# Modulation weights loaded in pieces whose partitions interleave two or four column blocks, in a fused two-model kernel

## The chip, the cores and the metric

The kernel runs on one core of a Trainium2 chip. The metric is the device time of one execution in microseconds (us). The core has a matrix engine (PE), a vector engine (DVE), a scalar engine (ACT), GpSimd (POOL) and a sync engine (SP) that issues most of the transfers (DMAs). The engines run beside each other and wait for each other on semaphores.

## The reference

Two transformer-like blocks follow each other on a sequence of 256 tokens of width 1024, in fp32. The first has two layers of feed-forward, token mixing and feed-forward; the second has one attention layer and one recurrent layer, each with a large feed-forward. What matters here is the modulation: every layer scales, shifts and gates its activations with vectors that come from one conditioning vector.

```python
c_act = jax.nn.silu(c)
mod = c_act @ ada_w[l] + ada_b[l]      # [1024] @ [1024, 9 * 1024]
sh1, sc1, g1, sh2, sc2, g2, sh3, sc3, g3 = jnp.split(mod, N_MOD, axis=-1)
h = modulate(rms_norm(x, norm_ffn1[l]), sh1, sc1)
# second block: 6 * 1024 columns a layer, for two vectors
mx = jnp.split((silu_c @ ada_w[i] + ada_b[i])[:, None, :], N_MOD_2, axis=-1)
mc = jnp.split(silu_cc @ ada_w[i] + ada_b[i], N_MOD_2, axis=-1)
```

Each of these products reads 1024 x 1024 weights for a segment (one `sh1`, `sc1` and so on), 4 MB, and uses every weight once for each vector.

## The kernel before

All weights pass through one stream of loads. `plan` lists the units (a unit is 1 MB of ordinary weights, mostly 1024 rows by 256 columns) in the order in which PE uses them, and `due` says before which unit each modulation segment must be complete. `build` cuts every segment into four pieces of 1 MB: 512 rows (four tiles of 128 rows) by 512 columns, first both row halves of the left 512 columns, then of the right. A budget over the units, with each unit's room, spreads the pieces between them; each piece costs as many steps as it has vectors. The result is `stream`, 271 units and 126 pieces.

SP walks through `stream` and loads each entry into one of four buffers `raw`, as soon as the entry four places before has been taken (semaphore `taken`). An ordinary unit is split in two parts: ACT copies it to the rounded high part `wh`, DVE subtracts to get the low part `wl`. PE then makes three products for each tile (high by high, high by low, low by high). ACT and DVE work up to two units ahead of PE.

A piece is handled on DVE alone (`take`, line 2108 for the multiply-add, line 2104 for the first step, a scale). For each of its four row tiles DVE adds, on every partition, the tile's 512 columns times that partition's element of the silu of the vector, into one of three sums `ACC` of 128 partitions by 512 columns. So a piece is four DVE steps for each vector, and a sum of 512 columns is complete after two pieces. For a few segments of the second block both vectors are taken in one pass.

PE then sums over the partitions (`flush`): four products, each with 128 columns of `ACC` as the weights and a column of ones as the moving side, give 512 results as four columns of the PSUM bank `PB[7]`. An fp32 product of this kind shows as two records in the trace. `summed` notes when a sum is complete and flushes older ones if more than three would be open, `spent` flushes after a unit until two are pending, and `mods` flushes all that a segment needs just before it is used. DVE then adds the bias (`mod`).

The start is special: of the first segment the right half is multiplied by PE itself (`direct_cols`), the small vectors are transposed by PE (the ring `su`) and copied by ACT, and then come the first three flushes, the first modulation and the first pair of units.

All helper calls of PE have line 623, those of DVE 2100 to 2108, those of ACT 1461 and 1462, the loads of SP line 568.

Of the kernel before, what the change touches and what calls it, by code (L numbers as in the profile page):

```python
# [27 lines left out]
K_MAIN = 385  # L28
K_R2, K_D0, K_D1, K_RD0, K_RD1, K_COS, K_SIN, K_BAND = 385, 513, 641, 769, 897, 1025, 1281, 1537
K_ALL = 2049  # L30
# [180 lines left out]

class Side:
# [24 lines left out]
def build(nc, t, out):  # L237
    units, due = plan(t)
    adas, direct = [], []
    for seg in sorted(due, key=lambda s: (due[s], s)):  # L240
# [3 lines left out]
        for i in range(4):  # L244
            src = w[512 * (i % 2):512 * (i % 2) + 512, s * 1024 + (i // 2) * 512:s * 1024 + (i // 2) * 512 + 512]
            if seg == (0, 0, 0):

                if i // 2:
                    direct.append(src)
                    continue  # L250
            adas.append((seg, i, vecs, due[seg], src))
# [13 lines left out]
    cost = np.cumsum([len(a[2]) for a in adas])  # L265
    ends = {}
    for a, c in zip(adas, cost):
        ends[a[3]] = c
    stream, ai, budget, sent = [], 0, 0.0, 0
    for i, u in enumerate(units):  # L270
        rate = max([(c - budget) / max(room[d] - room[i], 0.1) for d, c in ends.items() if d > i] + [0.0])
        budget = max(budget + max(rate, 0.0) * (room[i + 1] - room[i]), ends.get(i, 0))
        while ai < len(adas) and (cost[ai] <= budget + 1e-6 or adas[ai][3] <= i):
# [11 lines left out]
    for p, (kind, u) in enumerate(stream):  # L285
        seen[p % RAW] += 16 * (len(u[3]) if kind == "w" else 1)
# [3 lines left out]
        elif u[1] % 2:  # L290
            for v in u[2]:
                COLS_AT[(u[0][0], v, u[0][1], u[0][2])] = COLS_AT[None] = COLS_AT.get(None, 0) + 1
# [28 lines left out]
    with ExitStack() as ctx:  # L321
# [49 lines left out]
        IDB = sb("IDB", [128, 128], BF16)  # L371

# [21 lines left out]
        VR = [Y[:, i, 0:128] for i in range(4)]  # L394

# [105 lines left out]

        def smc(c, n):
# [45 lines left out]
        def _(e):  # L548
# [8 lines left out]
            for p, (kind, u) in enumerate(stream):  # L557
# [8 lines left out]
                parts = [(0, 4, 0, 512, u[4])] if kind == "a" else u[3]  # L566
                for k0, kn, c0, cn, src in parts:
# [35 lines left out]
        def _(e):  # L603
# [27 lines left out]
            def flush():  # L631

                p, v, i, key = pend.pop(0)
                E.wait_ge("taken", p + 1)
                E.wait_ge("mod", E.n["mod"])
                c0 = SEGCOL[key] + 4 * (i // 2)
# [4 lines left out]
                columns.append((key, c0))  # L641
                flushed[0] += 1

            def summed(places):
                for p in places:
                    kind, u = stream[p]
                    if kind == "a" and u[1] % 2 == 0:
                        acc[0] += len(u[2])
                        while flushed[0] < acc[0] - ACCS:
                            flush()  # L650
                    elif kind == "a":
                        pend.extend((p, v, u[1], (u[0][0], v, u[0][1], u[0][2])) for v in u[2])
# [802 lines left out]
        def _(e):  # L1455
# [104 lines left out]
            def ffn(l, seg, first=None):  # L1560
# [534 lines left out]
        def _(e):  # L2095
# [22 lines left out]
            def take(places):  # L2118

                for p in places:  # L2120
# [8 lines left out]
                    seg, i, vecs, _, _ = u  # L2129
                    view = raw_view(p)  # L2130
                    E.wait_ge(f"raw{p % RAW}", LAND[p])
                    E.wait_ge("su.read", 1)
                    base = sums_of[0]
                    for k in range(4):
                        for x, v in enumerate(vecs):
                            a = ACC[:, (base + x + 1) % ACCS, :]
                            col = 8 * v + 4 * (i % 2) + k
                            c = CV[:, col:col + 1]
                            if k == 0 and i % 2 == 0:
# [5 lines left out]
                            if k == 3 and v == vecs[-1]:  # L2145
# [4 lines left out]
                    if i % 2:  # L2150
                        sums_of[0] += len(vecs)
# [310 lines left out]
            E.step(e.memset(EPSC, EPS))  # L2462
            take(range(0, 3))
# [474 lines left out]
```

## Time and profile before

| | before |
|---|---|
| time, median of 3 runs | 2228.17 us (2224.69 to 2229.52) |
| span of the profiled execution | 2222.6 us |
| PE busy | 2155.5 us (97%) |
| DVE busy | 1674.6 us (75%) |
| ACT busy | 990.5 us (45%) |
| bytes moved | 417.47 MB, mean 188 GB/s |
| loads of modulation weights | 126 of 1 MB |

The profile is of one execution, and its span leaves out what lies around it, so it is compared with other spans. An engine's busy share is a mean over stages with different limits: the first feed-forwards carry many modulation pieces, the attention in the middle carries none. "Busy" for PE is modelled and hides gaps shorter than the length of a product, so a PE at 100% may still differ in pace.

### The profile page before, as it was taken

How to read it: one execution, taken by the hardware profiler on the slowest of the kernel's cores; microseconds unless marked ns; L12 is line 12 of the kernel's file. 1: busy time of each engine (PE TensorE's matmuls, PEld its weight loads, DVE VectorE, ACT ScalarE, POOL GpSimd, SP SyncE). 2: the span in 40 equal slices, each digit the busy share in tenths (PEclk: the TensorE clock that was granted, in tenths of full speed). 3: DMA queues.
4: the chain of work that ended last, by engine and by line, in shares of the span. 5: the costliest groups of instructions: out<-in, count | busy, mean ns of one | idle time of the engine just before them, and what ended most of it. 6: DMA issues, size and time to landing. Idle time of an engine off the chain costs nothing.

```text
span 2222.6 us, 36384 instructions
## 1 busy us (share of the span) xinstructions
PE 2155.5 (97%) x15539; PEld 1993.2 (90%) x15539; DVE 1674.6 (75%) x2327; ACT 990.5 (45%) x1331; POOL 31.1 (1%) x33
## 2 busy tenths in 40 slices
PE   7999999999999999999999899999999999999998
PEld 7999987999999998799998678888888887889998
DVE  6999877788798877778776774777776568987563
ACT  4534434534443443443344664422222348764442
POOL 0000000000000000000000000000000001110000
PEclk9999999999999999999999999999999999999999
DMA  9999744798789864467774102254465232133662
GB/s 322 317 330 309 248 133 150 242 316 298 264 284 305 302 202 153 142 196 248 236 228 142 36 4 74 80 186 155 156 221 189 76 114 69 48 122 127 223 191 76
DMA packets 338631, 417.47 MB, mean 188 GB/s; under 512 B 9274, under 2 KB 263208, under 8 KB 338472
## 3 DMA queue, kind: packets, MB, share of 16 engines
q1 hardware_dynamic: 335360, 411.84, 56.2%
q10 hardware_dynamic: 3112, 3.33, 0.5%
q8 instruction: 122, 2.00, 0.4%
q14 instruction: 37, 0.30, 0.0%
HBM read 414.09 MB, written 1.05 MB: 187 GB/s over the span
## 4 chain that ended last, share of the span: by engine, by line
PE 46%; DVE 7%; ACT 3%; issue 2%; POOL 0%; DVEq 0%; ACTq 0%
PE pb L623 45%; ACT wh L1461 1%; DVE wl L2100 1%; DVE T L2108 1%; PE pb L1289 1%; DVE ACC L2108 1%; DVE SM L2694 1%; DVE RS L2192 0%; DVE Hl L2108 0%; DVE L_y L2108 0%; ACT A_P L1935 0%; DVE L_y L2100 0%; ACT L_y L1462 0%; DVE L_y L2815 0%; DVE L_u L2108 0%
## 5 line engine op out<-in xcount | busy, mean ns | idle before, releaser
L623 PE MATMUL pb<-Hh,wh 128*128 128x256 f32 (+1 forms) x2624 | 795.5, 304 | 13.8 <-DVE wl L2100 5.4
L623 PE MATMUL pb<-Hl,wh 128*128 128x256 f32 (+1 forms) x2624 | 779.3, 297 | 0.0
L623 PE MATMUL pb<-Hh,wl 128*128 128x256 f32 (+1 forms) x2624 | 774.7, 297 | 0.0
L2100 DVE TENSOR_TENSOR wl<-raw,wh 128x2048 fp32r<-128x2048 f32 (+3 forms) x271 | 600.9, 2222 | 179.9 <-ACT wh L1461 179.1
L1461 ACT ACTIVATE wh<-raw 128x2048 fp32r<-128x2048 f32 (+3 forms) x271 | 502.2, 1855 | 357.6 <-PE pb L623 259.0
L623 PEld LDWEIGHTS pb<-Hh,wh 128*128 128x128 f32 x2624 | 504.6, 192 | 33.5 <-issue 9.6
L623 PEld LDWEIGHTS pb<-Hl,wh 128*128 128x128 f32 x2624 | 504.9, 192 | 15.3 <-issue 2.2
L623 PEld LDWEIGHTS pb<-Hh,wl 128*128 128x128 f32 x2624 | 501.9, 192 | 12.8
L623 PE MATMUL pb<-Bh,wh 128*128 128x256 f32 (+1 forms) x1376 | 420.1, 305 | 7.1 <-DVE Y L2100 2.5
L623 PE MATMUL pb<-Bl,wh 128*128 128x256 f32 (+1 forms) x1376 | 413.5, 300 | 0.0
L623 PE MATMUL pb<-Bh,wl 128*128 128x256 f32 (+1 forms) x1376 | 413.4, 300 | 0.0
L2108 DVE SCALAR_TENSOR_TENSOR ACC<-raw,SM,ACC 128x512 f32<-128x512 f32 x525 | 381.6, 750 | 18.1 <-DMA raw<-in_ada_w_dram 6.8
L623 PEld LDWEIGHTS pb<-Bh,wh 128*128 128x128 f32 x1376 | 263.3, 191 | 19.4 <-issue 6.4
L623 PEld LDWEIGHTS pb<-Bl,wh 128*128 128x128 f32 x1376 | 263.3, 191 | 9.3 <-issue 0.5
L623 PEld LDWEIGHTS pb<-Bh,wl 128*128 128x128 f32 x1376 | 263.2, 191 | 8.8
L1461 ACT ACTIVATE Bh<-T 128x512 fp32r<-128x512 f32 x92 | 58.1, 632 | 278.7 <-DVE T L2100 278.7
L1462 ACT ACTIVATE T<-pb 128x512 f32<-128x512 f32 x92 | 54.7, 595 | 159.0 <-PE pb L623 158.0
L2100 DVE TENSOR_TENSOR Bl<-T,Bh 128x512 fp32r<-128x512 f32 x92 | 63.7, 693 | 64.2 <-ACT Bh L1461 64.2
L2100 DVE TENSOR_TENSOR Y<-Y,pb 128x512 f32<-128x512 f32 x68 | 44.9, 684 | 58.7 <-PE pb L623 58.5
L623 PE MATMUL pb<-T,KM 128*128 128x256 f32 (+1 forms) x280 | 78.6, 408 | 3.9 <-ACT T L1462 3.9
L623 PEld LDWEIGHTS pb<-KM,ACC 128*128 128x128 f32 x600 | 74.0, 192 | 1.6 <-issue 0.5
L623 PE MATMUL pb<-KM 128*128 128x256 f32 x302 | 72.5, 390 | 0.0
(256 smaller groups left out, 2113.9 us busy)
## 6 DMA issues: line engine op xcount, KB each, us to landing
raw<-in_ada_w_dram SPq DMA_DIRECT2D x126, 1024.0 KB, 5.5
raw<-in_ffn_w_in_dram SPq DMA_DIRECT2D x88, 1024.0 KB, 6.7
raw<-in_mlp_w_dram SPq DMA_DIRECT2D x64, 1024.0 KB, 5.3
raw<-in_ffn_w_out_dram SPq DMA_DIRECT2D x32, 1024.0 KB, 6.5
raw<-in_mix_w_in_dram SPq DMA_DIRECT2D x22, 1024.0 KB, 5.7
raw<-in_ffn_w_out_dram SPq DMA_DIRECT2D x16, 768.0 KB, 4.6
raw<-in_attn_w_qkv_dram SPq DMA_DIRECT2D x12, 1024.0 KB, 6.2
raw<-in_lru_w_in_dram SPq DMA_DIRECT2D x10, 1024.0 KB, 5.1
```

Of the source, the lines that this page charges most:

```text
L623: return e.matmul(o, l, r, start=st, stop=sp, skip_group_check=True)
L1289: ins = e.transpose(p[:, c], A_P[:, 2 * (s % 2) + x, c], IDN)
L1461: return e.activation(o, i, func, scale=scale)
L1462: return e.activation(o, i, func, bias=bias, scale=scale)
L2100: return e.tensor_tensor(o, a, b, f)
L2108: return e.scalar_tensor_tensor(out=o, in0=a, scalar=s, in1=b, op0=f1, op1=f2)
L2694: E.step(e.tensor_reduce(S_NM2[:, h + x:h + x + 1], PB[S2[n % 2][x]][:, 0:nk], AXX, ALU.max))
```

## The change

A segment is now cut by rows first. A piece still has 1 MB, four `raw` rows of 512 columns on each of 128 partitions, but partition p holds column block p modulo q: with q = 2 both 512-column halves of one segment, with q = 4 the four halves of two neighbouring segments that are due at the same time. Piece i of 2q holds 512/q rows of the weights, and each of its tiles 128/q rows. It is loaded with q transfers, one for each block, to every q-th partition. All pieces of a segment (four) or of a pair (eight) go into one sum of 128 by 512, and PE's flush multiplies by q columns of marks (`K_BLK`, 1 where the partition belongs to the block) instead of one column of ones. The first two segments keep their old pieces (q = 1).

The vectors must be laid out in the same way, as `CW` with 144 columns: after its first small step DVE makes two copies that repeat each element q times, PE transposes six parts of 24 rows, and ACT applies the Silu while copying them to `CW`, after the first modulation. DVE waits for that copy before its first interleaved piece (`su.read` 10).

```diff
+K_BLK = {1: K_ONE, 2: 385, 4: 387}
+    for q in (2, 4):
+        k[p, K_BLK[q] + p % q] = 1.0
@@ build: the list of pieces
-        for i in range(4):
...
+        q = 2
+        if order and order[0] == (b, l, s + 1, *only) and due[order[0]] == due[seg]:
+            order.pop(0)
+            q = 4
+        for i in range(2 * q):
+            rows = w[512 // q * i:512 // q * (i + 1)]
+            adas.append(Piece(b, l, s, 0, q, i, vecs, due[seg], [rows[:, s * 1024 + 512 * j:s * 1024 + 512 * j + 512] for j in range(q)]))
@@ SP: loads
-                parts = [(0, 4, 0, 512, u[4])] if kind == "a" else u[3]
+                if kind == "a":
+                    n = 128 // u.q
+                    for j, src in enumerate(u.parts):
+                        e.dma_start(view[j::u.q, :, :], src.rearrange("(k p) n -> p k n", p=n)).then_inc(sems[f"raw{p % RAW}"], 16)
+                    continue
@@ PE: flush
+                blocks = KM[:, K_BLK[u.q]:K_BLK[u.q] + u.q]
                 for h in range(4):
-                    ins = mm(PB[7][:, c0 + h:c0 + h + 1], ACC[:, a, h * 128:h * 128 + 128], KM[:, K_ONE:K_ONE + 1], True, True)
+                    ins = mm(PB[7][:, c0 + h:c0 + h + 4 * u.q - 3:4], ACC[:, a, h * 128:h * 128 + 128], blocks, True, True)
@@ PE: summed (a sum opens with its first piece and is ready after its last)
-                    if kind == "a" and u[1] % 2 == 0:
+                    if kind == "a" and u.i == 0:
...
-                    elif kind == "a":
...
+                    elif kind == "a" and u.i == 2 * u.q - 1:
+                        pend.extend((p, v, u) for v in u.vecs)
@@ PE: start
+            E.wait_ge("dve.step", 3)
+            pw = fill("su")
+            for a in range(6):
+                z = VW4[:, 128 * a:128 * a + 128] if a < 4 else VW2[:, 128 * a - 512:128 * a - 384]
+                ins = e.transpose(pw[:, 24 * a:24 * a + 24], z, KM[0:24, K_ID:K_ID + 24])
+            full(ins, "su")
@@ ACT: after the first modulation
+                    act(CW[:, :], full("su")[:, 0:144], ACT.Silu).then_inc(sems["su.read"], 1)
@@ c_col: the column of the vector that belongs to tile kk of a piece
+            k, a = divmod(kk, q)
+            if q == 1:
+                return CV[:, 8 * v + k:8 * v + k + 1]
+            c = (0 if q == 4 else 96) + 24 * a + 8 * v + k
+            return CW[:, c:c + 1]
@@ DVE: take
-                    E.wait_ge("su.read", 1)
+                    E.wait_ge("su.read", 1 if u.q == 1 else 10)
...
-                            if k == 0 and i % 2 == 0:
+                            if k == 0 and u.i == 0:
                                 E.wait_ge("cols", base + x + 1 - ACCS)
                                 ins = ts(a, view[:, 0, :], c, None, ALU.mult, None)
@@ DVE: start
+            E.wait_ge("l_c", 64)
+            for q, z in ((4, VW4), (2, VW2)):
+                E.step(e.tensor_copy(z.rearrange("r (p q) -> r p q", q=q), VR[1][0:24, :].unsqueeze(2).to_broadcast([24, 128, q])))
```

## Rows read from the trace of the kernel before

**Rows 1.** Page, parts 1 and 5: busy us, instructions; mean ns of one

```profile
PE 2155.5 (97%) x15539; PEld 1993.2 (90%) x15539; DVE 1674.6 (75%) x2327; ACT 990.5 (45%) x1331; POOL 31.1 (1%) x33
...
L2100 DVE TENSOR_TENSOR wl<-raw,wh 128x2048 fp32r<-128x2048 f32 (+3 forms) x271 | 600.9, 2222 | 179.9 <-ACT wh L1461 179.1
```

**Rows 2.** Stretch: us; busy PE, PEld, DVE, ACT, POOL; clock, DMA, GB/s

```profile
94.00:181.00 87.00, 87.00 (x732) 87.00 (x731) 81.31 (x95) 35.59 (x30) 0.00 (x0) 1.00 0.98 330
181.00:250.00 69.00, 67.01 (x539) 66.39 (x539) 65.81 (x84) 27.26 (x27) 0.00 (x0) 0.98 0.92 307
...
410.00:611.00 201.00, 200.54 (x1665) 200.10 (x1666) 166.13 (x182) 80.92 (x69) 0.00 (x0) 1.00 0.89 299
611.00:835.00 224.00, 223.79 (x1856) 222.89 (x1855) 186.08 (x213) 97.83 (x93) 0.00 (x0) 1.00 0.82 273
```

**Rows 3.** Waits of 410 to 611 us: total, times, longest

```profile
ACT wh L1461 <- PE pb L623: 35.7, 10, 4.7
```

**Rows 4.** DVE's waits of 94 to 181 us; its scales on `ACC`

```profile
DVE Bl L2100 <- ACT Bh L1461: 3.5, 5, 0.7
DVE wl L2100 <- ACT wh L1461: 0.5, 1, 0.5
...
L2104 DVE TENSOR_SCALAR ACC<-raw,SM x12: 386/480/486, 98.9 to 242.3; 128x512 f32<-128x512 f32 x12
```

**Rows 5.** Timeline of PE, its first wait for `wl`

```profile
195.24 0.38 PE L623 MATMUL pb<-Hh,wh 128*128 128x256 f32 x1 [1.35 <-DVE wl L2100]
```

**Rows 6.** Instructions on the tile `ACC`, whole span

```profile
L623 PE MATMUL pb<-KM,ACC x600: 164/250/353, 33.5 to 2184.1; 128*128 128x1 f32 x150
L2108 DVE SCALAR_TENSOR_TENSOR ACC<-raw,SM,ACC x525: 740/752/769, 8.1 to 2168.6; 128x512 f32<-128x512 f32 x175
L2104 DVE TENSOR_SCALAR ACC<-raw,SM x75: 386/481/494, 7.6 to 2127.7; 128x512 f32<-128x512 f32 x75
```

**Rows 7.** Timeline of PE around a flush: start, length, what

```profile
335.14 0.28 PE L623 MATMUL pb<-wh,Hl 128*128 128x256 f32 x1
335.26 0.95 PE L623 MATMUL pb<-KM,ACC 128*128 128x1 f32 x8
...
336.27 0.28 PE L623 MATMUL pb<-wl,Hh 128*128 128x256 f32 x1
```

**Rows 8.** The same for PE's products on `ACC` alone; (x) counts records

```profile
94.00:181.00 87.00, 6.87 (x60) 1.00 0.98 330
181.00:250.00 69.00, 4.29 (x37) 0.98 0.92 307
...
410.00:611.00 201.00, 8.51 (x72) 1.00 0.89 299
611.00:835.00 224.00, 11.35 (x96) 1.00 0.82 273
```

**Rows 9.** Timeline of PE: the two flushes at the seam near 2000 us

```profile
2000.85 1.84 PE L623 MATMUL pb<-KM,ACC 128*128 128x1 f32 x16
```

**Rows 10.** Timelines of the start: PE, PE, ACT

```profile
26.96 0.63 PE L1105 MATMUL pb<-KM,Y 128*128 128x128 f32 x4
...
33.51 3.20 PE L623 MATMUL pb<-KM,ACC 128*128 128x1 f32 x24
...
51.50 0.60 ACT L1462 ACTIVATE T<-pb 128x512 f32<-128x512 f32 x1 [3.33 <-PE pb L623]
```

**Rows 11.** SP's issues of the gate weights, and their time to landing

```profile
1789.73 0.37 SPq L568 DMA_DIRECT2D raw<-in_lru_w_a_dram  x1
...
1791.17 0.47 SPq L568 DMA_DIRECT2D raw<-in_lru_w_i_dram  x1
...
DMA to landing us min/median/max: 2.8/3.3/3.7
```

**Rows 12.** SP's load of 1 MB just before them

```profile
DMA to landing us min/median/max: 5.4/5.4/5.4
```

**Rows 13.** DMA rate of 0 to 222 us in 40 slices

```profile
GB/s 145 387 376 387 387 359 348 163 287 378 357 291 364 139 288 365 324 358 323 361 281 368 342 362 340 281 372 273 374 311 367 360 225 369 191 339 347 209 374 306
```

More of the change, by code:

```diff
@@ L1 @@
 import itertools
-from collections import defaultdict
+from collections import defaultdict, namedtuple
 from contextlib import ExitStack
@@ L27 @@
 K_ID, K_ONE, K_R1, K_INVF = 0, 128, 256, 384
-K_MAIN = 385
-K_R2, K_D0, K_D1, K_RD0, K_RD1, K_COS, K_SIN, K_BAND = 385, 513, 641, 769, 897, 1025, 1281, 1537
-K_ALL = 2049
+K_BLK = {1: K_ONE, 2: 385, 4: 387}
+K_MAIN = 391
+K_R2, K_D0, K_D1, K_RD0, K_RD1, K_COS, K_SIN, K_BAND = 391, 519, 647, 775, 903, 1031, 1287, 1543
+K_ALL = 2055
 def constants():
@@ L209 @@
 LO_FULL = {j: 2 * LO_STEPS.index((j, 1)) for j in range(4)}
+Piece = namedtuple("Piece", "b l s half q i vecs due parts")
 class Side:
@@ L239, in build @@
     adas, direct = [], []
-    for seg in sorted(due, key=lambda s: (due[s], s)):
+    order = sorted(due, key=lambda s: (due[s], s))
+    while order:
+        seg = order.pop(0)
         b, l, s, *only = seg
@@ L243, in build @@
         vecs = only or ([0] if b == 0 else ([1, 2] if l == 0 or s < 2 else [1]))
-        for i in range(4):
-            src = w[512 * (i % 2):512 * (i % 2) + 512, s * 1024 + (i // 2) * 512:s * 1024 + (i // 2) * 512 + 512]
-            if seg == (0, 0, 0):
-                if i // 2:
+        if seg in ((0, 0, 0), (0, 0, 1)):
+            for i in range(4):
+                src = w[512 * (i % 2):512 * (i % 2) + 512, s * 1024 + (i // 2) * 512:s * 1024 + (i // 2) * 512 + 512]
+                if s == 0 and i // 2:
                     direct.append(src)
                     continue
-            adas.append((seg, i, vecs, due[seg], src))
+                adas.append(Piece(b, l, s, i // 2, 1, i % 2, vecs, due[seg], [src]))
+            continue
[6 more added lines that the diff above has]
+            adas.append(Piece(b, l, s, 0, q, i, vecs, due[seg], [rows[:, s * 1024 + 512 * j:s * 1024 + 512 * j + 512] for j in range(q)]))
     at_unit = [ROOM.get(u[0], 1.0) for u in units]
@@ L264, in build @@
     room = np.concatenate([[0.0], np.cumsum(at_unit)])
-    cost = np.cumsum([len(a[2]) for a in adas])
+    cost = np.cumsum([len(a.vecs) for a in adas])
     ends = {}
     for a, c in zip(adas, cost):
-        ends[a[3]] = c
+        ends[a.due] = c
     stream, ai, budget, sent = [], 0, 0.0, 0
@@ L272, in build @@
         budget = max(budget + max(rate, 0.0) * (room[i + 1] - room[i]), ends.get(i, 0))
-        while ai < len(adas) and (cost[ai] <= budget + 1e-6 or adas[ai][3] <= i):
+        while ai < len(adas) and (cost[ai] <= budget + 1e-6 or adas[ai].due <= i):
             stream.append(("a", adas[ai]))
@@ L285, in build @@
     for p, (kind, u) in enumerate(stream):
-        seen[p % RAW] += 16 * (len(u[3]) if kind == "w" else 1)
+        seen[p % RAW] += 16 * len(u[3] if kind == "w" else u.parts)
         LAND.append(seen[p % RAW])
@@ L289, in build @@
             POS.append(p)
-        elif u[1] % 2:
-            for v in u[2]:
-                COLS_AT[(u[0][0], v, u[0][1], u[0][2])] = COLS_AT[None] = COLS_AT.get(None, 0) + 1
+        elif u.i == 2 * u.q - 1:
+            for v in u.vecs:
+                COLS_AT[None] = COLS_AT.get(None, 0) + 1
+                for s in range(u.s, u.s + (2 if u.q == 4 else 1)):
+                    COLS_AT[(u.b, v, u.l, s)] = COLS_AT[None]
     START, SECOND = POS[0] + 1, POS[1] + 1
@@ L631, in flush @@
             def flush():
-                p, v, i, key = pend.pop(0)
+                p, v, u = pend.pop(0)
                 E.wait_ge("taken", p + 1)
                 E.wait_ge("mod", E.n["mod"])
-                c0 = SEGCOL[key] + 4 * (i // 2)
+                c0 = SEGCOL[(u.b, v, u.l, u.s)] + 4 * u.half
                 a = (flushed[0] + 1) % ACCS
+                blocks = KM[:, K_BLK[u.q]:K_BLK[u.q] + u.q]
                 for h in range(4):
-                    ins = mm(PB[7][:, c0 + h:c0 + h + 1], ACC[:, a, h * 128:h * 128 + 128], KM[:, K_ONE:K_ONE + 1], True, True)
+                    ins = mm(PB[7][:, c0 + h:c0 + h + 4 * u.q - 3:4], ACC[:, a, h * 128:h * 128 + 128], blocks, True, True)
                 ins.then_inc(sems["cols"], 1)
-                columns.append((key, c0))
+                for j in range(u.q):
+                    columns.append(((u.b, v, u.l, u.s + j // 2), c0 + 4 * j))
                 flushed[0] += 1
@@ L2144, in take @@
                                 ins = stt(a, view[:, k, :], c, a, ALU.mult, ALU.add)
-                            if k == 3 and v == vecs[-1]:
+                            if k == 3 and v == u.vecs[-1]:
                                 ins.then_inc(sems["taken"], 1)
```

19 lines of the change are left out of this document (10 added, 9 removed).

## The prediction

> **What bounds the kernel now.** I read the page's busy shares first: PE is busy for 2155.5 of 2222.6 us [rows 1], so PE is the likely bound. A share averages over stages, so the table of stretches comes next [rows 2]. In 410 to 611 us PE is busy 200.54 of 201 us and ACT waits for PE, because its buffers are full [rows 3]: PE sets the pace. In 94 to 181 us PE is just as full, but DVE is busy 81.31 of 87 us, and of its 5.7 us of idle time the largest named part is the hand-over of hidden values from ACT, 3.5 us [rows 4]. DVE never waits for PE there. At 195.24 us PE at last waits 1.35 us for DVE's low half `wl` [rows 5]. In 181 to 250 us DVE is busy 65.81 of 69 us. So from about 94 to 250 us DVE paces the kernel just behind PE, and the reader should see that PE time saved there is not time saved. The profiled execution spans 2222.6 us; the median of the timed runs, 2228.17, is 5.6 us above it, and I carry those 5.6 us over unchanged.
>
> **What is removed on PE.** A sum that is ready in `ACC` costs four fp32 products, eight records [rows 6]. In the stream this is 335.14 to 336.27 us from the matmul before to the second one behind, 1.13 us where two steps of 0.12 would be 0.24: 0.89 us a flush [rows 7]. The 600 records are 75 flushes. For after I go through the planner's list of segments, where two neighbours with one due time become a pair. The first two segments keep their 3. In the rest of the first block, segments 2, 5 and 8 stay alone and (3,4) and (6,7) pair up in both layers, and (0,1) in layer 1: 11. The context columns (0,1) ahead of time: 1. The second block: (0,1) 1, segment 2 twice (two vectors), (3,4) twice, 5 twice, next layer (0,1) twice, (2,3), 4 and 5 once each: 12. Together 3 + 11 + 1 + 12 = 27. So 48 flushes vanish, 48 x 0.89 = 42.7 us of PE time.
>
> Each remaining flush has q = 2 or 4 columns of block marks instead of one column of ones. Records of one column and of 256 columns alike follow each other at about 0.12 us [rows 7], so 2 or 4 columns lie between two equal prices and cost nothing more.
>
> **Where the flushes lie.** PE flushes when more than two sums are pending, or when a segment is asked for. With half as many sums or fewer, most now wait until they are asked for. Of the 75, 3 lie at the start, 8 in four pairs at seams, where PE waits for squares from ACT in any case (one of the pairs: 16 records at 2000.85 us [rows 9]), and 64 inside matmul streams. After: 3 at the start, 11 at seams, 13 inside. The cover of a seam flush is the square and copy that ACT makes of the last tile; were it gone, 11 - 8 = 3 more flushes there cost 2.7 us. Inside streams 64 - 13 = 51 flushes fall away, 45.4 us. Of these, 94 to 250 us holds 60 + 37 records, 12 flushes [rows 8], of which 2 stay. The 10 that go are worth 8.9 us of PE time but nothing in time, because DVE paces that stretch. What is left: 41 x 0.89 = 36.5 us.
>
> **What is added on DVE.** The count of multiply-adds is the same, 600. But a sum's first step was a scale of 481 ns (75 of them) and is otherwise a multiply-add of 752 ns [rows 6]; 48 of them change, 48 x 0.27 = 13 us spread over the run. Where PE paces, DVE has room (166.13 of 201 us busy [rows 2]) and this costs nothing. In 94 to 250 us 12 sums began [rows 4] and 3 will: 9 x 0.27 = 2.4 us straight on the path. Just as close to a limit are the parts of 410 to 835 us with the most modulation work; PE's saving pushes DVE's share in 410 to 611 us from 83% to some 86%, more in its densest parts, and DVE reached 93 to 95% when it paced. I take 1.5 us off, bounds 0 and the 14 us of a rival below.
>
> **What is added at the start.** Two small copies on DVE fit in its first wait for data. PE makes six more transposes ahead of the direct columns; four there take from 26.96 to about 27.4 us, 0.12 each [rows 10], so 0.7 us. They need a bank that ACT frees after its first copy of the vectors, perhaps 0.2 us, and PE's three flushes at 33.51 us [rows 10] end the chain to the first modulation: 0.7 us on the path, bounds 0 and 1.5. DVE's later wait for the copied `CW` has nothing late in it: ACT's one Silu falls before 51.50 us, where ACT has waited 3.33 us for PE [rows 10].
>
> **What moves in the queues.** A piece keeps its 1 MB and its runs of 2 KB, but becomes 2 or 4 transfers of 64 or 32 partitions. SP's issues take 0.37 to 0.47 us, so a piece's last part goes out 0.4 to 1.4 us later. The nearest row is the unit of gate weights, four 256 KB transfers on all partitions: first issued 1789.73, last 1791.17, each landed within 3.7 us, so the unit was in after at most 5.2 us [rows 11], where one 1 MB transfer took 5.4 [rows 12]. So no loss in a quiet queue. Behind a piece on SP stands the next unit's weight load; in the busy stretch DVE frees buffers 2.2 us apart or more, the time of one `wl` [rows 1], longer than four issues. No row shows transfers of 32 partitions spaced by four. Bounds: nothing, or half speed (first rival). I take 1.5 us, nearer to the gate weights' row.
>
> The Trainium skill ("DMA: Bandwidth & Descriptors", Measured and Rules for kernel authors) speaks against the change: at least 1 MiB a transfer for 75% of peak, and disjoint partition halves gain nothing because they serialize. By its fit of 2.0 us plus bytes at 436 GB/s, an estimate, four parts in strict sequence would take 10.4 us instead of 4.4; the gate weights' row disagrees, since the parts overlap. The same skill ("SBUF — State Buffer", Door 1) says that bandwidth follows how many of 16 ports the partitions reach, and every fourth partition reaches all; no row here shows it.
>
> **The sum.** 36.5 - 2.4 - 1.5 - 0.7 - 1.5 = 30.4, rounded down to 29 for seam flushes that may not hide wholly: span 2193.6, time 2199.
>
> **Rivals.** (1) The parts collide: several DMA engines write to the same few partitions' port at once, and a piece moves at c times the time of now. In 94 to 181 us the queues are 98% busy at 330 GB/s, a weight unit and a piece every 6.4 us [rows 2]. The best slices reach 387 GB/s [rows 13], 2.7 us a MB. A pair then takes 2.7 x (1 + c), over 6.4 from c = 1.35. At c = 2 each of 24 pieces in 94 to 250 us adds 1.75 us, 42 us. In 410 to 835 us 121 MB take 313 us at best, the 42 pieces add 114: 427 us instead of 425, so the 16 flushes saved there bring nothing and 2 us are lost. The other 25 flushes still bring 22 us. Total 2228 + 44 - 22 + 1 = 2251. It turns slower than before from about c = 1.9, where 65 x (c - 1.35) equals the 36 us gained. For it: the busy queues; against: equal bytes and run length, and four parts in a row that cost nothing.
> (2) The front end (DVE, with ACT's weights late from DMA) paces 410 to 835 us too once PE is quicker: 16 x 0.89 = 14 us less, 2213. For it: DMA share 0.89 and 0.82; against: ACT waits for PE 35.7 us in 410 to 611 [rows 3].
> (3) All inner flushes are gained, because DVE's pace was partly PE's: 2228 - 45.4 + 0.7 = 2184. Against it: PE's wait at 195 us.
> (4) The change does less than it says: a middling collision, c near 1.8, eats the gain: within 0.2%.
>
> **How the numbers follow.** This kernel can be told from no change beyond about 0.2%, 4.5 us. Forecast 0.58; rival 1 0.14, rival 2 0.14, rival 3 0.06, rival 4 0.08. Faster: 0.58 + 0.14 + 0.06 = 0.78; same 0.08; slower 0.14. The range runs from rival 3, 2185, to the edge of rival 4, 2226, and leaves out rival 1 and some of 4.
>
> **What would show it.** `ACC` products on PE: 216 records, not 600. Stretches after 250 us shorter by 0.89 us for each flush gone; the first 250 us not shorter, perhaps 3 longer, with more PE waits for `wl`. DVE's scales on `ACC`: 27. Landing of pieces near 6 to 7 us in the busy stretch if the queues bear it, 9 and more with DVE waiting for `raw` if they collide. I would be wrong if 32-partition transfers are slow, or if seams wait for the late flushes.

## Result and profile after the change

| | before | after |
|---|---|---|
| time, median of 4 runs each, on one chip | 2226.43 us (2220.85 to 2229.52) | 2211.52 us (2206.09 to 2214.35) |
| ratio, with its 95% interval | | 0.994 (0.9921 to 0.9959) |
| span of the profiled execution | 2222.6 us | 2203.6 us |

The change gains about 15 us. The forecast was 29. The time lies inside the range and the sign is the one forecast, but half of the gain is missing, and most of what follows asks where it went. All figures are from fast runs; one run of the kernel before, at 6412.82 us with a granted clock of 0.326, is left out throughout.

The page of the kernel after, parts 1, 5 and 6; after the bar: busy us, mean ns of one, and idle time before; the loads' last number is the median time from issue to landing in us.

```profile
PE 2119.4 (96%) x15161; PEld 1953.9 (89%) x15161; DVE 1686.0 (77%) x2325; ACT 991.5 (45%) x1332; POOL 31.8 (1%) x33
...
L654 PE MATMUL pb<-KM,ACC 128*128 128x2 f32 (+2 forms) x216 | 27.3, 251 | 1.7 <-DVE ACC L2148 1.7
...
raw<-in_ffn_w_in_dram SPq DMA_DIRECT2D x88, 1024.0 KB, 7.3
raw<-in_ada_w_dram SPq DMA_DIRECT2D x320, 256.0 KB, 4.1
```

PE has 36.1 us less work than in [rows 1], and the products on `ACC` are 216, as forecast. The first block's feed-forward weights (`in_ffn_w_in`) landed 6.7 us after their issue before and take 7.3 now.

The stretches that answer to [rows 2] (same columns):

```profile
94.00:181.00 87.00, 82.46 (x667) 81.50 (x667) 80.33 (x92) 33.28 (x26) 0.00 (x0) 0.98 0.96 324
181.00:250.00 69.00, 60.10 (x479) 58.98 (x478) 65.62 (x84) 27.09 (x26) 0.00 (x0) 0.98 0.90 303
410.00:611.00 201.00, 200.43 (x1657) 199.71 (x1656) 174.12 (x193) 86.94 (x77) 0.00 (x0) 1.00 0.89 299
611.00:835.00 224.00, 222.62 (x1821) 219.52 (x1820) 191.54 (x217) 98.83 (x91) 0.00 (x0) 1.00 0.86 285
```

In the first two rows PE was busy 87.00 and 67.01 us; now it is busy 82.46 and 60.10, while DVE is as full as it was. Freed PE time turned into waiting there. In the last two rows PE is still full: it paces, and what it saved is time saved.

Waits of 94 to 250 us in the kernel after (us in total, times, longest):

```profile
PEld pb L654 <- DVE wl L2140: 14.5, 10, 3.0
PE pb L654 <- DVE wl L2140: 8.7, 7, 2.8
```

Before, the same two came to 1.6 us on PEld (the weight loads) and 1.3 us on PE, the one at 195 us [rows 5].

To see where time is won and lost I laid the executions on top of each other: for each unit of weights, when PE starts on it, and how much later or earlier that is than in the profiled execution of the kernel before. The last columns are for experiments below. "Again" is another profiled execution of the same kernel.

| PE starts unit | before at | before again, twice | after | after again | pieces whole (a4_whole) | late interleaving | again |
|---|---|---|---|---|---|---|---|
| 2, first block | 54.0 | -0.9, -0.6 | +0.4 | +0.3 | +7.7 | +0.9 | +0.5 |
| 8 | 94.6 | -0.9, -0.6 | +0.1 | -0.5 | +6.9 | +0.9 | +0.5 |
| 33 | 249.7 | 0.0, +1.7 | +7.1 | +7.0 | +9.5 | +3.6 | +2.6 |
| 85 | 605.1 | 0.0, +1.7 | -2.6 | 0.0 | +0.1 | -3.2 | -6.1 |
| 120 | 815.3 | -0.1, +1.7 | -8.2 | -6.1 | -6.2 | -9.0 | -12.3 |
| 177, second block | 1209.3 | -1.6, +0.1 | -13.2 | -12.7 | -9.4 | -15.5 | -18.5 |
| 216 | 1709.0 | +1.1, +2.9 | -16.8 | -16.4 | -14.4 | -18.9 | -19.5 |
| 270, last | 2159.4 | -0.6, +1.1 | -18.5 | -18.1 | -16.1 | -20.7 | -21.3 |

The kernel after loses 7 us between units 8 and 33, in 94 to 250 us, and then wins 25.6 to the end. Between these two units executions of the kernel before differ by up to 2.3 us (0, +0.9 and +2.3), so 7 is well outside. What was expected of the two further executions of the kernel before:

> The kernel before, looked at once more, to see how far PE's start of each unit moves between two executions of one kernel. If the first 250 us repeat within 1 us, the 2 to 3 us that most variants lose between 169 and 250 us are an effect of their edits; if they move by 2 to 3 us, that much is the spread of a stretch whose loads are late, and only the 7 us of the changed kernel are more.

### The profile page after: what moved, and what is told of

The parts are those of the page before. It is cut to its first block, busy times and chain, and to the rows that moved or that the text cites. A ratio compares the mean times of both kernels' runs of the same rounds, so it can differ in the third digit from the quotient of the medians.

```text
span 2203.6 us, 35914 instructions
## 1 busy us (share of the span) xinstructions
PE 2119.4 (96%) x15161; PEld 1953.9 (89%) x15161; DVE 1686.0 (77%) x2325; ACT 991.5 (45%) x1332; POOL 31.8 (1%) x33
## 4 chain that ended last, share of the span: by engine, by line
PE 44%; DVE 9%; ACT 3%; issue 2%; POOL 0%; DVEq 0%; ACTq 0%
PE pb L654 43%; DVE ACC L2148 2%; ACT wh L1500 1%; DVE wl L2140 1%; PE pb L1328 1%; DVE T L2148 1%; DVE SM L2735 0%; DVE Hl L2148 0%; DVE RS L2230 0%; DVE L_y L2148 0%; DVE T L2140 0%; DVE L_y L2140 0%; ACT L_y L1501 0%; DVE L_y L2856 0%; DVE L_u L2148 0%
## 5 line engine op out<-in xcount | busy, mean ns | idle before, releaser
L654 PEld LDWEIGHTS pb<-Hh,wl 128*128 128x128 f32 x2624 | 500.3, 191 | 12.7
L2148 DVE SCALAR_TENSOR_TENSOR ACC<-raw,CW,ACC 128x512 f32<-128x512 f32 x552 | 400.2, 749 | 10.8
L1501 ACT ACTIVATE Hh<-T,MOD 128x256 fp32r<-128x256 f32 x104 | 49.4, 504 | 42.3 <-DVE T L2148 42.3
```

What stands on the lines that cost most here:

```text
L654: return e.matmul(o, l, r, start=st, stop=sp, skip_group_check=True)
L1501: return e.activation(o, i, func, bias=bias, scale=scale)
L2148: return e.scalar_tensor_tensor(out=o, in0=a, scalar=s, in1=b, op0=f1, op1=f2)
```

## The experiments

All ratios are to the kernel before on the same chip. "Early loss" is how much later unit 33 starts, less the same of unit 8.

**The split of the pieces, alone** (measured twice). The kernel before; only the loads are cut.

```diff
+                if kind == "a" and p > 5:
+                    for j in range(4):
+                        e.dma_start(view[j::4, :, :], u[4].rearrange("(k p) n -> p k n", p=128)[j::4, :, :]) ...
```

> The kernel before with one thing added: every modulation piece from the seventh stream entry on is loaded with four transfers, each to every fourth partition, with the same bytes to the same places. Layout, sums, flushes and scales are those of before. Theory 1 (the split transfers cost the time that the changed kernel lost in its first 250 us, 7 us there): weights land later behind the split pieces, 8 us instead of 7 from issue to landing in 94 to 250 us, DVE waits for the high halves, and the last unit of that stretch (start 249.7 before) starts 4 to 6 us later; the whole is 4 to 8 us slower, ratio 1.002 to 1.0035. Theory 2 (the multiply-add starts and the start's extra work cost it): nothing lands later that anyone waits for, within 1 us of before.

> The split over every fourth partition once more, beside the other three splits: 1.002 to 1.004 if its cost repeats.

Measured: 1.0032 (1.0014 to 1.005) and 1.0024 (1.0012 to 1.0037), early loss 4.0 and 8.0 us; after unit 33 the two executions keep the same distance to the end, within 2 us. Splitting costs 5 to 7 us by the ratios, and in the profiles all of it falls where the front end (loads, ACT, DVE) paces, and nothing where PE does.

**The split undone.** The kernel after, with each piece in one transfer. What lands then no longer fits the interleaved layout, so its sums mix rows and columns of the weights.

```diff
-                    for j, src in enumerate(u.parts):
-                        e.dma_start(view[j::u.q, :, :], src.rearrange("(k p) n -> p k n", p=n)) ...
+                    e.dma_start(view, u.parts[0].rearrange("(k p) n -> p k n", p=128)) ...
```

> The changed kernel with each piece loaded by one transfer of 1 MB, as before the change (the data then does not fit the interleaved layout: rows and columns of the weights are left mixed up). Everything else is the changed kernel. Theory 1 (split transfers): 5 to 8 us faster than the changed kernel, so 20 to 23 us faster than before, ratio 0.990; weights land in 7 us again in 94 to 250 us, and the last unit there starts 2 to 3 us later than before instead of 7. Theory 2 (starts and start-up): as the changed kernel, ratio 0.993 to 0.994.

Measured: 0.9935 (0.9915 to 0.9955). The early loss falls from 7 us to 2.6, near the spread of the kernel before: theory 1 holds for the early loss. But the ratio is the one of theory 2: the time hardly moves, 2209.47 us against 2211.42 for the kernel after on the same chip. Its profile starts with unit 2 already 7.7 us late, before any interleaved piece; that surprise is taken up below.

**DVE's longer first steps**, alone and undone. Both kernels leave out parts of their sums or add to what was there.

```diff
 a3_starts, in the kernel before:
-                                ins = ts(a, view[:, 0, :], c, None, ALU.mult, None)
+                                if opens(seg[0], seg[1], seg[2], i):
+                                    ins = ts(a, view[:, 0, :], c, None, ALU.mult, None)
+                                else:
+                                    ins = stt(a, view[:, 0, :], c, a, ALU.mult, ALU.add)
 d2_scales, in the kernel after:
+                            elif k == 0 and u.i % 2 == 0:
+                                E.wait_ge(*mine[v])
+                                ins = ts(a, view[:, 0, :], c, None, ALU.mult, None)
```

> The kernel before, where 48 of the sums' first steps on DVE are multiply-adds instead of scales, as many and about at the places where the change makes them so; they add to what the sum held, so the modulation vectors come out of wrong sums. Nothing else moves. Theory A (the prediction's): DVE paces 94 to 250 us, 9 of these steps lie there, 2.4 us longer, ratio 1.001, and nothing elsewhere. Theory B (DVE's longer steps are a good part of the 7 us that the changed kernel loses before unit 33, since a later hand-over of wl goes back into the queues): 5 us or more, ratio 1.002 and up. Theory C: hidden, within 0.5 us.

> The changed kernel, where the first step of every second piece of a sum is a scale again, as many scales as in the kernel before (75); what the sum held is lost there, so the modulation vectors are wrong. Theory A (DVE's longer starts are 2.4 us of the 7 us lost by unit 33, and the split loads the rest): unit 33 comes 4 to 5 us behind the kernel before instead of 7, and the time is 2 to 2.5 us less than the changed kernel's: ratio 0.993. Theory B (only the queues are late there, DVE's steps lie in the shadow of late loads): unit 33 stays 7 us behind, ratio 0.994 to 0.995. Theory C (DVE is the bound alone): all 7 us come back, ratio 0.991.

Measured: 1.001 (0.9997 to 1.0022), early loss 2.1 us, no more than the kernel before shows by itself; and 0.9931 (0.9907 to 0.9955), early loss 7.5 us. Giving DVE its short steps back returns nothing of the early loss. What DVE saved it waited instead. Its wait for ACT in the stretch from unit 8 to unit 33, first in the kernel after (94 to 257 us), then in d2_scales (101 to 265 us):

```profile
DVE wl L2140 <- ACT wh L1500: 2.7, 6, 1.2
```

```profile
DVE wl L2140 <- ACT wh L1500: 5.3, 7, 1.2
```

That is 2.6 us more, where nine short steps save 2.4. So the early loss speaks for theory B of the second text: the steps lie in the shadow of late loads. The ratio alone can't tell, since 0.9931 is what theory A had. The profile of d2_scales also won 32.2 us after unit 33, and not 25.6; it had 34 us at the lower of PE's two clock levels (1.2 of 2.4 GHz) between unit 33 and the last, where the kernel after had 44. Work at half the clock loses half of its time at most, here 5 of the 10 us, and that is most of the difference. No run separates this from an effect of the steps.

**Why the split costs.** Three other ways to cut the same piece, beside the two measurements above.

```diff
 e3_tiles:     view[:, j:j + 1, :]        four transfers, each to all 128 partitions
 e4_quarters:  view[32 * j:32 * j + 32]   four transfers, each to 32 neighbours
 e5_two:       view[j::2, :, :]           two transfers, even and odd partitions
```

> The kernel before, where each piece from the seventh on is loaded in four transfers of 256 KB, one for each row tile, so that every transfer goes to all 128 partitions. Undoing the split gave back most of the changed kernel's early loss; SP's issues took 2.6 us for a piece of four there. Theory N (the number of transfers costs: issues and packets): as slow as the split over every fourth partition, ratio 1.002 to 1.004, SP busy near 2.6 us a piece. Theory G (the shape costs: 32 partitions a transfer): SP's four issues take 1.6 us as those of the gate weights, landing as before, ratio 1.000 to 1.001.

> The kernel before, where each piece from the seventh on is loaded in four transfers to 32 neighbouring partitions each. Theory I (the interleaving costs: partitions four apart): faster than the split over every fourth partition, ratio 1.000 to 1.001. Theory G (32 partitions a transfer cost, wherever they lie): the same as that split, 1.002 to 1.004. Theory P (neighbouring partitions share a port and collide): slower than it, 1.01 or more, pieces landing 9 us or more after their issue.

> The kernel before, where each piece from the seventh on is loaded in two transfers, to the even and the odd partitions. If the cost of the split goes with the number of transfers, half of it: ratio 1.001 to 1.002, SP's two issues 1.3 us. If it is only the place where SP's issues come to more than the 2.2 us between two buffers set free, nothing: 1.000.

| | ratio | early loss | SP's issues of one piece | weights of the first block land after |
|---|---|---|---|---|
| one transfer (before) | 1 | 0 to 2.3 us | 0.37 us | 6.7 us |
| two, every second partition | 0.9998 (0.9984 to 1.0012) | 0.3 | 1.28 | 7.1 |
| four, one for each row tile | 0.9993 (0.9979 to 1.0008) | 2.8 | 1.75 | 7.2 |
| four, every fourth partition | 1.0024 and 1.0032 | 8.0 and 4.0 | 2.6 | 7.5 |
| four, 32 neighbours each | 1.0832 (1.0783 to 1.0881) | 69.6 | 1.74 | 12.1 |

SP's timeline of three kernels, about 163 to 175 us (start, duration of all issues, what, count). First the kernel before:

```profile
169.85 0.37 SPq L568 DMA_DIRECT2D raw<-in_ada_w_dram  x1
172.05 0.37 SPq L568 DMA_DIRECT2D raw<-in_ffn_w_in_dram  x1
```

The kernel after:

```profile
169.79 2.54 SPq L596 DMA_DIRECT2D raw<-in_ada_w_dram  x4
172.38 0.59 SPq L599 DMA_DIRECT2D raw<-in_ffn_w_in_dram  x1
```

And two transfers a piece (e5_two):

```profile
163.54 1.28 SPq L568 DMA_DIRECT2D raw<-in_ada_w_dram  x2
165.74 0.38 SPq L572 DMA_DIRECT2D raw<-in_ffn_w_in_dram  x1
```

An issue to every second or fourth partition takes 0.64 us, one to all partitions or to neighbours 0.44. Two of the first kind, or four of the second, end before the next buffer is free, 2.2 us after the first issue, and cost nothing that can be measured. Four of the first kind take 2.6 us: the weights behind the piece go out at +2.6 instead of +2.2, their own issue takes 0.59 us instead of 0.37, and ACT waits for weights (35.6 us for `in_ffn_w_in` in 94 to 250 us of the kernel after, 31.1 before). So the cost seems to have a threshold, and not to go by the number of transfers. Some 24 pieces at 0.4 us would be 10 us if every one counted; 4 to 8 were seen. This reading is an inference from the first four rows of the table, which agree with it. SP was not delayed by itself, so a slower transfer of the strided parts (the weights land after 7.5 us with it and 7.2 with row tiles) is not excluded.

The last row of the table is the collision of rival 1, in pure form. Slices of its page in this stretch move 221 to 242 GB/s where the kernel before moves 330 [rows 2], at the same byte count, with the DMA engines counted as busy throughout. Its waits in 94 to 250 us:

```profile
ACT wh L1465 <- DMA raw<-in_ffn_w_in_dram: 72.2, 12, 12.0
```

The Trainium skill ("SBUF — State Buffer", Door 1: The DMA port swizzle) says that the bandwidth of a transfer goes by how many of 16 ports its partitions reach. These runs agree: 32 neighbours cost 8.3%, 32 partitions spaced by four 0.2 to 0.3% at equal size. The Trainium skill ("DMA: Bandwidth & Descriptors", Rules for kernel authors) advises against two transfers to disjoint partition halves, because they serialize. Here even and odd halves neither gained nor lost: 0.9998.

**The price of a flush.** The kernel before; 48 of the flushes are cut from four fp32 products to one of four columns, so three quarters of their sums are left out.

> The kernel before, in which 48 of the 75 flushes, those that the change does without, make one product with four columns of ones instead of four products with one (their sums are left out). Loads and DVE's work are those of before. It takes 48 x 0.67 = 32 us of PE time away, three quarters of what the change takes. Theory A (my sum: PE's time inside matmul streams after 250 us is time, flushes at 94 to 250 us are free): 40 x 0.67 = 27 us faster, ratio 0.988. Theory B (PE's time comes back as waits for DVE and lower granted clock, whatever the loads do): 12 to 16 us faster, ratio 0.993 to 0.9945, with as many or more low-clock spells as the changed kernel.

Measured: 0.9912 (0.9887 to 0.9936), 19 us, between the figures of the two theories. PE's start of the last unit comes 25.8 us earlier in the profile, and unit 33 gained nothing. Between these two units the flushes took 23.8 us less. The profile won more than that, 26.7 us, because it was an execution with a high clock: 27 us at the lower level there, where the kernel before had 37 (the mean over the span, as a share of full speed, is 0.991 against 0.987). Up to half of these 10 us is clock and not flushes. So the flushes are worth about what their rows say, where PE paces. And again the median of the runs moved less than the profile: their mean clock was 0.9870, that of the kernel before on this chip 0.9896.

**Two blocks everywhere.** The kernel after with q = 2 throughout: two transfers a piece, 39 flushes.

> The changed kernel with two blocks in every interleaved piece and no pairs of segments: 39 flushes instead of 27, two transfers a piece instead of four. Theory A (each flush has its price of 0.89 us wherever PE paces, and two or four transfers cost the same): 12 more flushes, 2 of them in 94 to 250 us where they cost nothing, so 9 us slower than the changed kernel: ratio to before 0.998 to 1.000. Theory B (the number of transfers is what costs, and half as many give back half of the 7 us by unit 33): 5 us slower at most, ratio 0.995 to 0.9975, and unit 33 only 3 to 4 us behind the kernel before.

Measured: 0.9935 (0.9919 to 0.9952), level with the kernel after. Early loss 3.8 us instead of 7, and 20.9 us won after unit 33 instead of 25.6. The ratio lies below both forecasts, theory B's being nearer, and it had unit 33 right. Twelve flushes more and a lighter split about cancel.

**Late interleaving** (measured twice). The kernel after, but the first layer's segments 0 to 7 and the early context columns keep old pieces, so nothing is split or merged before 250 us.

```diff
-        if seg in ((0, 0, 0), (0, 0, 1)):
+        if ((b, l) == (0, 0) and s < 8) or only == [2]:
```

> The changed kernel, with the interleaving begun later: segments 0 to 7 of the first layer and the early context columns keep their old pieces (one transfer to all 128 partitions, one block), so that no piece is split in the stretch of 94 to 250 us, where DVE paces. From segment 8 of the first layer on it is the changed kernel. Theory T1 (the pieces' split costs time only where queues and DVE are the bound, 7 us by unit 33 in the changed kernel, and merging saves nothing there): PE reaches unit 33 within 1.5 us of the kernel before, keeps the later gain, and ends 24 to 27 us ahead of the kernel before: ratio 0.988 to 0.991. Theory T2 (the gain that is missing was lost later, to more spells of low granted clock and to waits; PE's lead at unit 33 is worth nothing, as the seams take it back): as the changed kernel, 0.993 to 0.996.

> The late interleaving once more: does its lead on the changed kernel (2 to 3 us in the first look at it, within the intervals) repeat? Theory T1: ratio to before 0.989 to 0.992 and a lead on the changed kernel in the same call of 2 us or more. If it is chance, the two kernels' ratios meet at 0.993 to 0.995.

Measured: 0.9907 (0.9884 to 0.9931) and 0.992 (0.9895 to 0.9946), early loss 2.7 and 2.1 us. The kernel after had 0.994 and, measured again, 0.9946 (0.9925 to 0.9966), for which the text was:

> The changed kernel once more, on the chip of the other three, to compare with them: ratio 0.9925 to 0.9955. If the granted clock explains the spread of its runs, the slower runs are those with the lower mean clock, about 1 us for each 0.0005.

The ratios are those of T1: not doing the change where DVE paces is some 6 us better than doing it. Each interval overlaps that of the kernel after, which ran on other chips; the difference rests on all ten runs of each kernel. Of T1's marks in the profile two were missed. Unit 33 came 2.7 and 2.1 us late and not within 1.5, and the end 21 us ahead and not 24 to 27.

**A fourth sum**, on top of that. In the kernel after, PE waits for one of a pair of sums that DVE has only just finished:

```profile
1462.94 0.39 PE L654 MATMUL pb<-Hh,wl 128*128 128x512 f32 x1
1465.06 1.05 PE L654 MATMUL pb<-KM,ACC 128*128 128x2 f32 x8 [1.73 <-DVE ACC L2148]
```

With three sums, two new ones can't be opened until one of this pair is flushed.

> The late interleaving with four sums in ACC instead of three, so that a new pair of sums never forces PE to flush a pair that DVE has only just finished (PE's wait of 1.73 us near 1465 us in the changed kernel, with a spell of 3.4 us at the low granted clock behind it). If that wait and its spell are lost time, 1.7 + 1.7 us go: 3 us less than the late interleaving with three sums, ratio lower by 0.0013 to 0.0015, and no low clock near 1467 us. If the wait only takes the place of a later one (at the next seam), the same time within 1 us.

Measured: 0.9916 (0.9893 to 0.994). The wait is gone, and at unit 198 the profile was 3.1 us further ahead (each taken from its own unit 2), but by unit 216 it was 1.0 us behind three sums. No gain: the second expectation.

**The clock.** Whole pieces, two blocks, the fourth sum and the short first steps (d2_scales) all had profiles in which unit 2 was 7 to 8 us late. So I set the mean granted clock of every timed run beside its time. In 87 runs of the kernel before the time falls by 1.7 us for each 0.001 of mean clock (correlation -0.90).

| | runs | mean granted clock | median us |
|---|---|---|---|
| before, all chips | 87 | 0.9890 | 2224.2 |
| after | 10 | 0.9826 | 2211.5 |
| pieces whole | 6 | 0.9822 | 2209.5 |
| late interleaving | 10 | 0.9858 | 2205.5 |
| the change's start alone | 12 | 0.9866 | 2230.6 |
| late interleaving with two idle products | 4 | 0.9880 | 2201.8 |

0.9890 to 0.9826 is 0.0064, by that slope 11 us: the greater part of the missing 14. The slope is a correlation within one kernel, and to carry it over to others is an estimate. Two kernels search for the place.

```diff
 f2_start, in the kernel after (every segment gets old pieces):
-        if seg in ((0, 0, 0), (0, 0, 1)):
+        if True:
 f1_warm, in the late interleaving:
+            stay(1, 1)
             E.wait_ge("dve.step", 3)
...
             full(ins, "su")
+            stay(1, 1)
```

> The change's start alone: the two copies on DVE, PE's six transposes of 24 rows, the Silu into CW and the longer constants, with every piece, sum and flush of the kernel before. In four of eight profiles of kernels with this start a spell of 17 to 21 us at half the granted clock begins about 1.5 us after these transposes, in none of ten profiles of the old start; such a spell puts the first pair of units 7 us later, and over 10 runs the changed kernel's mean granted clock is 0.9826 against 0.9891 of the kernel before. Theory S (the start makes those spells, by itself): mean granted clock 0.987 to 0.988, single runs 7 us apart, 2 to 5 us longer in the median, ratio 1.001 to 1.002. Theory T0 (they come from elsewhere in the change): the clock as before, ratio within 1.0005.

> The late interleaving with two more idle products of PE at the start, one before its wait for DVE's copies and one behind the six small transposes, to keep PE's work dense there. Theory S (thin work at the transposes sets off the spell at half clock): no such spell, mean granted clock 0.987 or more (0.9858 without them), 0.5 us longer for the products and 2 to 3 us shorter for the clock: ratio 0.989 to 0.9905. Theory T0: the clock stays at 0.986, the ratio between 0.9907 and 0.992 or a little above.

Measured: the start alone costs 1.0022 (1.0008 to 1.0036), 4.6 us, where the forecast had 0.7. The two idle products (PE works on constants for about 1 us in all) bring the late interleaving to 2201.76 us, 0.9893 (0.9876 to 0.9909). Theory S is near in both. The start alone lowered the mean clock to 0.9866, from 0.9885 for the kernel before on its chip. That is 0.0019 of the 0.0064 that the kernel after lost; no run shows where the rest comes from.

What the idle products do is less certain. The interval overlaps those of the late interleaving, which ran on other chips. The profile reaches unit 2 2.7 us late, where the late interleaving without them was 0.9 and 0.5 us late, and wins its lead only after unit 33. And two of the ten runs without them, at a clock of 0.990, took 2196 and 2197 us, less than any with them.

The stretch of 24 to 54 us, in which the columns are those of [rows 2]; first the start alone, then with the idle products:

```profile
24.00:54.00 30.00, 29.86 (x150) 27.31 (x150) 18.54 (x35) 9.36 (x15) 0.00 (x0) 0.66 0.67 220
```

```profile
24.00:54.00 30.00, 29.69 (x196) 27.52 (x195) 22.47 (x36) 11.72 (x17) 1.24 (x1) 0.89 0.83 276
```

A granted clock of 0.66 means that two thirds of these 30 us ran at the lower level, 1.2 of 2.4 GHz. What stands ahead of it on PE, in the fourth-sum kernel, which has the same start:

```profile
26.34 0.63 PE L1138 MATMUL pb<-KM,Y 128*128 128x128 f32 x4
27.11 0.52 PE L1143 MATMUL pb<-KM,Y 24*128 24x24 f32 x6
27.56 1.10 PE L654 MATMUL pb<-SM,D_w 128*128 128x1 f32 x8
28.52 2.05 PE L654 MATMUL pb<-KM 128*128 128x256 f32 x4
30.37 1.71 PE L654 MATMUL pb<-SM,D_w 128*128 128x1 f32 x8
```

The four idle records take 2.05 us instead of 1.11: the clock fell at 28.4 us, 1.3 us after the first of the six small transposes, around which PE stands still for some tenths of a microsecond. The executions without the spell have the same gaps in this place, so it sets in or not with the same work. That the transposes, and not the copies or the Silu of the new start, bring it on is read from the place alone. Of nine profiles with this start and without the idle products five have this spell, 17 to 21 us long, 7 us lost each; of ten with the old start none has. With the idle products it was absent in the one profile taken, and the clock of the four runs (0.987 to 0.989) gives no sign of it; four of nine profiles lacked it without them too.

## Why the prediction was half right

The path and the price of a flush were right. The steps that failed are three terms of the sum. The start was put at 0.7 us and measured 4.6 (1.8 to 8.0). The split of the pieces was put at 1.5 us and cost 5 to 7. And the sum had no term for the granted clock at all ("I carry those 5.6 us over unchanged"): its mean fell from 0.9890 to 0.9826, some 11 us by the slope above, part of which is the start's. That the time fell inside the range says little, since the edges are those of rivals 3 and 4; and the 2.4 us taken off for DVE, which no run shows, cancelled a part of the error by luck.

**PE paces after 250 us, DVE before.** Right, and the stretches above show it. The signs named held: 216 records, 27 scales, PE waiting for `wl`, the first 250 us longer. They were to be 3 us longer; it was 7.

**A flush costs 0.89 us.** Right. One flush of the kernel after with its neighbours:

```profile
466.63 0.28 PE L654 MATMUL pb<-Hh,wl 128*128 128x256 f32 x1
...
466.75 0.95 PE L654 MATMUL pb<-KM,ACC 128*128 128x2 f32 x8
...
467.56 0.36 PE L654 MATMUL pb<-Bh,wh 128*128 128x256 f32 x1
...
467.76 0.28 PE L654 MATMUL pb<-Bl,wh 128*128 128x256 f32 x1
```

From 466.63 to 467.76 is 1.13 us, to the hundredth what it was with a column of ones [rows 7]. Two or four columns cost nothing more.

**How many flushes count: 41.** Too many by 3: after unit 33, 60 flushes became 22, so 38 went. Up to the start of the last unit, where the table ends, it is 58 and 21. Each with what it delays behind it, the flushes there took 55.7 us of PE before and 22.9 after, 32.8 saved and not 36.5. The extra ones at the seams are not hidden under squares: those at 262, 374 and 402 us took 1.0 us each. I had rounded by 1.4 us for this, and it needed 3.7.

**32.8 us saved, 25.6 arrived.** What PE saves in a stretch, it does not always keep at the seam behind it. The wait for a `Y`, ahead of the product that opens a seam, over 1600 to 1730 us of the kernel after:

```profile
PE pb L654 <- DVE Y L2140: 3.6, 2, 2.3
```

and of the kernel before:

```profile
PE pb L623 <- DVE Y L2100: 1.8, 2, 0.9
```

1.8 us are given back here, and 1.3 where PE waits for `M_g` in the mixing stages (2.7 before, 4.0 after); the wait for the pair at 1465 us is inside the 22.9. The rest, 4 us, is about half of the 7 us more at the low clock (44 us against 37 between the two units). These waits are the ones that grew; PE's whole idle time there grew by 4.0 us with the 1.7 at 1465 us in it, so other waits shrank by almost 1 us. This ledger was read from profiles and not tested one by one.

**DVE's longer starts: 2.4 us.** Nothing is seen of it: undone, they return nothing of the early loss, and DVE waits 2.6 us longer for ACT instead. DVE was full in that stretch, but behind loads that came late: ACT waited 60 us for feed-forward weights there, and 51 in the kernel before. "DVE is 93% busy" was not "DVE is the bound". A spread of 2.3 us between executions leaves some doubt. Of the 1.5 us for DVE's dense parts in 410 to 835 us no run tells: from unit 51 to 120 PE won 12.5 of the 14.0 us of flushes.

**The split: 1.5 us.** Wrong by 4 to 5 us, if the issue reading above holds. I had the right criterion, four issues against the 2.2 us between two buffers set free, and the wrong duration: 0.37 to 0.47 us an issue, read from transfers to all partitions [rows 11, 12], where issues to every fourth partition take 0.64. Rival 1 priced a collision of ports. It exists, at 32 neighbours, and the interleaving of this change escapes it.

**The start: 0.7 us, bounds 0 and 1.5.** Wrong, the most clearly mis-sized term: 4.6 us, because in five of nine profiles with this start the granted clock falls by half for 17 to 21 us just behind the six transposes. I had counted instructions and not the clock.

**The sum.** Span 2193.6 was forecast and 2203.6 came. Its execution had no long spell at the start: 25.6 us won after unit 33 less the 7.1 by which unit 33 was late is 18.5 us ahead at the last unit, and its timed run, 2206.09 us, was the fastest of four. For the median, with each term where the runs put it: 32.8 for flushes, less 3.1 given back at seams, less some 5.5 for the split, less 4.6 for the start, gives 19.6; what remains to the median of 15 is about the 4 us more at the low clock after 250 us. The terms come from different runs, each with 2 to 3 us of doubt, so that they close is no proof. They overlap with the 11 us by clock, which is a second way of cutting the same loss, not a further one.

**The rivals.** Rival 2 (the front end paces 410 to 835 us too) is out: PE won 12.5 us from unit 51 to 120, for flushes worth 14.0. Rival 3 is out by the early waits. Rival 4 is out, as the gain is 0.6% and not within 0.2; nor did the parts collide. The fastest version is the late interleaving with idle products, 2201.76 us, against 2211.4 for the kernel after, on another chip and by ratios 0.9893 and 0.9946.

**Open.** Where the greater part of the lost clock goes, and why whole pieces, which lose little early, run at a clock as low as 0.9822; whether the start's transposes could go elsewhere for nothing; and why the same split lost 4 us in one execution and 8 in the other.

## What to carry to other kernels

Before spreading an edit over a whole kernel, cut it by stage: it pays where the relieved engine paces, and can cost where the edit's by-products (issues, small products) meet the bound. Price an issue by the shape that you mean to use, and compare the sum of a burst of issues with the time between two buffers set free: here bursts below it cost nothing measurable, and the one above it cost 5 to 7 us. If a change moves PE's work, set the mean granted clock of all runs beside their times; here a loss of 0.006 goes with some 11 us, as much as a dozen flushes.

## What was not expected of the hardware

- Four transfers to 32 neighbouring partitions each made the kernel 8.3% slower, with the feed-forward weights landing after 12.1 us in the median instead of 6.7; the same bytes to every fourth partition cost 0.2 to 0.3%.
- An issue on SP took 0.37 us for 1 MB to all partitions, 0.44 for 256 KB to all or to neighbours, and 0.64 for strided partitions.
- Six transposes of 24 rows (0.52 us) were followed, in five of nine profiles, by 17 to 21 us at half the granted clock; with about 1 us of idle products around them it was absent in the one profile taken. The Trainium skill ("TensorE: Matmul & The Clock Gate", HAM oscillation) tells of a clock lowered by idle gaps of PE; here the gap was a fraction of a microsecond beside thin work, in a PE that the profile shows as 29.86 of 30 us busy.
